# A hybrid decoder step on one core: how the sparse layer's lists are exchanged, and in which order its engines work

## The reference, cut to what matters

```python
q, k, v, iq, ik, iw = _split(h @ W['w_in_c'][j], C_SPLITS)
q = _rope(q.reshape(B, T, HC, DHC), pos)          # 8 heads of 128
k_rows = _rope(k.reshape(B, T, KVC, DHC), pos)    # 2 heads of 128
...
isc = jax.nn.relu(jnp.einsum('bthd,bsd->bths', iqb, ik_all))
isc = jnp.einsum('bths,bth->bts', isc, iwb)
isc = jnp.where((k_pos[None, :] <= qp[:, None])[None], isc, -jnp.inf)
top, sel = lax.top_k(isc, topk)                   # 256 of 1032 keys for a sample's token
...                                               # softmax attention over the chosen keys only
y = o.reshape(B, T, HC * DHC) @ W['w_out_c'][j]
```

## Time and profile before

| what | value |
|---|---|
| three runs | 2281.42, 2282.49 (median), 2288.36 us |
| the profiled execution | 2288.35 us, its span 2286.6 us |
| TensorE busy | 2117.3 us, 93% of the span |
| VectorE, ScalarE, POOL busy | 1233.7, 708.4, 269.7 us |
| chain that ended last, by engine | TensorE 72%, VectorE 12%, issue 5%, weight loads of TensorE 5%, ScalarE 3%, transfers 2% |
| mean granted clock of TensorE | 0.98 of full speed |

### The profile page before, as it was taken

One profiled execution on the slowest core, in us unless ns is written; L12 is line 12 of the kernel. 1 busy time (PEld: TensorE's weight loads), 2 busy tenths in 40 slices (PEclk: granted clock), 3 DMA queues, 4 the chain that ended last, 5 costly groups with the idle time before them and its releaser, 6 DMA issues.

```text
span 2286.6 us, 37435 instructions
## 1 busy us (share of the span) xinstructions
PE 2117.3 (93%) x15226; PEld 1873.6 (82%) x15230; DVE 1233.7 (54%) x2035; ACT 708.4 (31%) x1085; POOL 269.7 (12%) x243
## 2 busy tenths in 40 slices
PE   8988899898999999999998998888998999999997
PEld 6755697688878999999996576668976999999996
DVE  4367376855353566336634898564443466525642
ACT  5244334423231322212234424342322322212222
POOL 0022003431000000000003235220000100000001
PEclk9999999989999999999999999999999999999998
DMA  5378323314442222222224125642343222222221
GB/s 185 116 235 276 98 74 122 120 51 139 174 150 87 74 84 75 83 74 84 70 76 128 54 74 171 189 125 80 125 166 124 75 75 83 75 83 80 78 73 56
DMA packets 220861, 249.28 MB, mean 109 GB/s; under 512 B 18498, under 2 KB 175436, under 8 KB 220486
## 3 DMA queue, kind: packets, MB, share of 16 engines
q1 hardware_dynamic: 199162, 196.22, 27.1%
q0 software_dynamic: 9936, 28.78, 3.9%
q10 hardware_dynamic: 11592, 21.88, 2.8%
HBM read 233.63 MB, written 13.00 MB: 108 GB/s over the span
## 4 chain that ended last, share of the span: by engine, by line
PE 72%; DVE 12%; issue 5%; PEld 5%; ACT 3%; DMA 2%; PEldq 1%; POOL 0%; SPq 0%; DVEq 0%; POOLq 0%; ACTq 0%
PE PS L831 50%; PE PS L888 5%; PE PS L810 4%; PEld PS L831 2%; PE PS L1255 1%; PE PS L1270 1%; DVE arena L3202 1%; DVE arena L3200 1%; DVE arena L3235 1%; DVE arena L3232 1%; PE PS L1442 1%; DVE arena L2434 1%; PEld PS L1133 1%; PEld PS L810 1%; DVE stat L2527 1%
## 5 line engine op out<-in xcount | busy, mean ns | idle before, releaser
L831 PE MATMUL PS<-hT_r,WH 128*128 128x288 f32 (+2 forms) x1856 | 554.0, 298 | 21.7 <-issue 17.1
L831 PE MATMUL PS<-xr_r,WH 128*128 128x288 f32 (+2 forms) x1920 | 570.3, 297 | 1.6 <-POOL W_r L658 1.6
L831 PE MATMUL PS<-hT_r,W_r 128*128 128x288 f32 (+2 forms) x1856 | 549.5, 296 | 0.0
L2391 DVE TENSOR_TENSOR W_r<-W,WH 128x1024 fp32r<-128x1024 f32 (+1 forms) x219 | 284.2, 1317 | 373.0 <-ACT WH L1706 372.1
L831 PE MATMUL PS<-arena_r,WH 128*128 128x224 f32 (+2 forms) x1920 | 439.4, 297 | 3.7 <-issue 3.7
L1706 ACT ACTIVATE WH<-W 128x1024 fp32r<-128x1024 f32 (+1 forms) x262 | 266.1, 1034 | 504.6 <-PE PS L831 279.0
L831 PEld LDWEIGHTS PS<-hT_r,WH 128*128 128x128 f32 x1856 | 350.2, 189 | 35.0 <-issue 31.6
L831 PEld LDWEIGHTS PS<-xr_r,WH 128*128 128x128 f32 x1920 | 362.9, 189 | 2.3 <-issue 2.3
L831 PEld LDWEIGHTS PS<-hT_r,W_r 128*128 128x128 f32 x1856 | 350.3, 189 | 0.0
L831 PEld LDWEIGHTS PS<-arena_r,WH 128*128 128x128 f32 x1920 | 325.0, 189 | 6.4 <-issue 6.3
L831 PE MATMUL PS<-arena_r,W_r 128*128 128x288 f32 (+2 forms) x704 | 208.7, 296 | 0.0
(11 more groups left out here) (439 smaller groups left out, 3056.6 us busy)
## 6 DMA issues: line engine op xcount, KB each, us to landing
W<-in_w_ffn_in SPq DMA_DIRECT2D x176, 256.0 KB, 3.3
W<-in_w_ffn_out SPq DMA_DIRECT2D x40, 512.0 KB, 3.5
W<-in_w_in_ab SPq DMA_DIRECT2D x28, 512.0 KB, 3.6
C<-in_cache_mem_k SPq DMA_DIRECT2D x10, 1024.0 KB, 7.8
C<-in_cache_diff_k POOLq DMA_DIRECT2D x32, 256.0 KB, 3.9
C<-in_cache_diff_k SPq DMA_DIRECT2D x32, 256.0 KB, 3.4
C<-in_cache_diff_v POOLq DMA_DIRECT2D x32, 256.0 KB, 5.1
C<-in_cache_diff_v SPq DMA_DIRECT2D x32, 256.0 KB, 5.0
```

Source lines behind the costliest of these rows:

```text
L831: ins = mm(o, w[:, k, c * 128:c * 128 + 128], v(k0 + k)[:, t0:t1], start=opens and first and k == 0 and e == 0, stop=last and k == nk - 1 ...
L2391: v_.tensor_tensor(slot_view(WL, NW, n), slot_view(W, NW, n), plain(slot_view(WH, NV, n)), ALU.subtract).then_inc(lo_done, 1)
```

## The change

It touches only the order of work and the waits of the sparse stage.

1. `swap_lists` goes from POOL to SP, ahead of the first slot of the output weights, and so behind the first three key blocks. POOL makes its low halves without a stop.
2. The new keys are rotated after 18 rounds, not after 22.
3. ScalarE: `cp_turned(a + 1)` ahead of `cp_exp(a + 2)`.
4. VectorE: in the turns that load keys, the first key copy stands ahead of `cp_max(a)`, where that is there; the low half of an output slot (`ahead`) is made in the middle of the next turn, not at a turn's end, and there is one fewer before the end.
5. The barrier is gone. TensorE waits for all copies of turned tiles (`wait_tr`) and, at chunk 6 of the first block, for VectorE's last copy of values; ScalarE waits for its stores and for the last values before it fetches the memory keys. `align(NBANK, 3)` gives the first block the upper three of six banks.

```diff
 (SP)
+            def swap_lists():
+                sp.wait_ge(handoff["lists"], 1)
+                for e in range(2):
+                    sp.dma_start(L["tops_other"][64 * e:64 * e + 64], L["tops"][64 - 64 * e:128 - 64 * e]).then_inc(swapped, 16)
+
             for kind, n in LOADS:
                 if kind == "w":
+                    if n == first_slot["c_out"]:
+                        swap_lists()
...
 (POOL; the same function is taken away there)
                     a, z = POOL_RUNS[1]
-                    rests(a, z - 3)
-                    swap_lists()
-                    rests(z - 3, z)
+                    rests(a, z)
...
 (TensorE)
             cp_values(4 * (NB // 2) - 1, last)
-            barrier()
+            wait_tr()
             tj.use(6, 7)
-            project_features("c_out", oX_c, "D")
+            pj.align(NBANK, 3)
+
+            def pair_ready(k):
+                if k == 6:
+                    pe.wait_ge(handoff["p_copied"], DP + 4 * (NB // 2))
+
+            project_features("c_out", oX_c, "D", pair_ready)
...
 (ScalarE)
                     cs_keys(1, range(1), "DA")
+                cp_turned(a + 1)
                 cp_exp(a + 2)
-                cp_turned(a + 1)
...
-            barrier()
             tj.use(6, 7)
+            pj.align(NBANK, 3)
+            act.wait_ge(stores, 16 * S["stores"])
+            act.wait_ge(handoff["p_out"], DP + 4 * (NB // 2))
             fetch_memory(1)
...
 (VectorE)
-            largest(6, 22)
+            largest(6, 18)
...
-            largest(22, 32).then_inc(handoff["lists"], 1)
+            largest(18, 32).then_inc(handoff["lists"], 1)
...
-            def cs_keys(bb, groups, whos):
+            def cs_keys(bb, groups, whos, halves=range(2)):
                 for g in groups:
-                    for half in range(2):
+                    for half in halves:
...
                 a, more = 4 * p, p + 1 < NB // 2
+                if more:
+                    cs_keys(0, range(1), "DA", range(1))
                 if p:
                     cp_max(a)
                 if more:
-                    cs_keys(0, range(2), "DA")
+                    cs_keys(0, range(1), "DA", range(1, 2))
+                    cs_keys(0, range(1, 2), "DA")
...
                 cp_max(a + 1)
+                if p:
+                    ahead(first_slot["c_out"] + p - 1)
...
-                ahead(first_slot["c_out"] + p)
                 cs_turned(p)
             cp_copy(4 * (NB // 2) - 1)
-            barrier()
+            pj.align(NBANK, 3)
```

More of the change, by code:

```diff
@@ L659, in rests @@
                                             ALU.subtract).then_inc(lo_pool, 1)
[L661 to L664, removed]
             def sample_states():
```

## The result

The changed kernel took **2267.94 us** in the median of six runs (2265.68 to 2276.94), the kernel before, in the same rounds, 2286.12 (2281.42 to 2288.36): a ratio of **0.9938, 95% interval 0.9919 to 0.9958**. It is faster by 0.6%, and 2268.7 was forecast. The profiled execution took 2267.56 us, its span 2265.8, with a mean granted clock of 0.983.

A forecast was written before the change was run, and what follows sets the result against it. TensorE at its projections was taken as the bound, so only its standstills pay. Terms -8.0 + 1.0 - 5.4 + 2.0 - 1.5 - 1.9 gave -13.8 us, a forecast median of 2268.7 us, range 2264.5 to 2276.

The forecast's parts named there:

- The swap leaves POOL: Values' projection: TensorE loses its 4.06 us wait for POOL and 3.1 us of slow clock, together 7.2 us.
- the swap on SP: SP's queue: swap issued behind twelve key loads at 1427.9, lists in time, merge 0.5 us in place of 5.17.
- Rival B: List merge on VectorE is slow by itself, reading one list backwards; in all -8.6, 2273.9 us; chance 0.07.
- New keys rotated sooner: TensorE's new-key turn: rotating four rounds sooner saves 3.6 us of wait and slow clock; the rotation takes some 10 us.
- Start of the loop: Sample scores start at 1439.2, not 1447.22, after TensorE waits 2.8 us for the selection: -8.0 us.
- The clock's +1.0: Before the sample scores, TensorE's wait can lower the clock: 0 to +2.5 us, +1.0 taken.
- part 5: Attention loop: ScalarE's copies ahead of the next exponentials save 1.35 us in each of four turns, -5.4 us.
- VectorE's key copy first: Turns 1 and 2: maximum, exponentials and ScalarE's key copy come 1.0 us later, +2.0 us for both.
- The split moved: VectorE's weight split goes into a wait for keys, saving 0.8 us at two borders; taken as -1.5 us.
- no barrier: Before the output projection, TensorE's 2.09 us standstill nearly goes: -1.9 us.
- Rival D: Slower: the clock stays low through the loop after the wait before the sample scores; 2292 us; chance 0.04.
- E: Whole kernel: no change to be told, gains and losses cancel to within 6.8 us; chance 0.07.

The follow-up runs named there:

- experiment 2: Changed kernel with the new keys rotated after 22 rounds again, not 18; 2273.42 us, ratio 0.9950 to the kernel before.
- experiment 11: Changed kernel with the new keys rotated after 9 rounds, not 18, and nothing else; 2269.28 us, ratio 0.9930 to the kernel before.
- experiment 3: Changed kernel with ScalarE's exponentials of the next job ahead of its copies again; 2279.54 us, ratio 0.9973 to the kernel before.
- experiment 5: Changed kernel with VectorE's weight split back at the end of each turn; 2274.23 us, ratio 0.9947 to the kernel before.
- experiment 6: Changed kernel with the barrier back at the sparse stage's end and the align calls gone; 2273.70 us, ratio 0.9942 to the kernel before.
- experiment 4: Changed kernel with VectorE's maximum ahead of the first key copy again; 2270.99 us, ratio 0.9938 to the kernel before.
- experiment 9: Changed kernel measured again without an edit, the second execution; 2270.30 us, ratio 0.9922 to the kernel before.
- experiment 7: Kernel before with only the loop's edits: swap on POOL, new keys after 22 rounds; 2279.28 us, ratio 0.9964 to the kernel before.
- experiment 1: Changed kernel with the list swap back on POOL, ahead of its last three low halves; 2282.38 us, ratio 0.9976 to the kernel before.

## Why the prediction was right, step by step

1. *The swap leaves POOL* (7.2 us for TensorE) and 3. *the swap on SP.* Right. TensorE no longer stands in the projection, the swap is issued at 1423.13, just behind the twelfth key load, and the merge takes 0.42 us where 0.5 was expected. With parts 1 and 2 together TensorE was ready for the sample scores 10.1 us sooner, and 10.7 in the second execution (10.8 forecast). Rival B is out: the same instruction took 0.42 or 0.43 us beside an idle POOL (the eight executions, of seven kernels, that have the swap on SP behind the twelfth key load), 1.53 where one half that began at 1419.31 still ran, and 4.98, 5.17 and 5.32 beside three in a row. The reading of the merge as work plus waiting was taken from one pair of rows; it held.

2. *New keys rotated sooner.* Right in price (3.8 to 4.1 by experiment 2, 3.6 taken) and in course: start at 27.34 (27.4 forecast), 9.44 us long (10), lists 3.1 us later than before (4.1). The lists were then ready 1.87 us ahead of SP (1421.26 against 1423.13), so that their lateness was hidden, as said, and experiment 11 shows it from the other side.

4. *Start of the loop.* -8.13 us against -8.0, and -7.5 to -7.8 in the six other executions that start alike. TensorE waited 1.93 us for the selection in the profiled execution; the others waited 2.74 to 2.90 (2.8 forecast).

   **The clock's +1.0 is the term that was mis-sized.** The effect exists, but not in every execution. Seven executions have a wait of 2.74 to 2.90 us ahead of the sample scores. Four of them (experiments 3, 5, 6 and 11) have a stretch at 0.5, the 1.2 GHz level, that begins at the sample scores, and a turn 0 longer by 0.8 to 1.6 us; three (experiments 2, 4 and 9) have none. The profiled execution, with the shorter wait, had none either.

   What the sum put at nothing is the other low stretch, the one 6 to 11 us behind the start of the kernel before. It is gone: turn 0 lost 3.06 us, of which about 1.55 is part 5's copies and the other 1.5 the clock. In place of +1.0 stands -1.5, for this pair of executions. This stretch is there in both traces that have both of the old waits (the kernel before and experiment 7) and in none of the other eleven. With one of the two alone it is absent (experiment 1 has the wait for POOL, experiment 2 that in the new keys' turn). So it seems to go with the old start, but with one or two traces of each kind this is not shown.

5. *ScalarE's copies.* Predicted 1.35 a turn, measured 1.5: 3.53 less 1.98 is 1.55, and experiment 3 gives 1.52 and 1.52. For four turns -6.1 instead of -5.4.

6. *VectorE's key copy first.* Predicted +1.0 for each of turns 1 and 2, measured +0.94 and +0.98, by the mechanism named: the maximum, the exponentials and ScalarE's key copy shift in a row, and TensorE waits 1.79 us for the last.

7 and 8. *The split moved, no barrier.* -1.5 and -1.9, -3.4 together. Turn 1 is 0.57 shorter, which the copies and the key copy explain alone (-1.55 + 0.94). Turn 2 is 1.23 shorter: -1.55 + 0.98 leaves -0.66 for the split. Turn 3 is 4.19 shorter: -1.55 and another -0.66 leave -1.98 for the end. The sum of both parts is so -3.3. How the end divides was wrong: the barrier alone is 0.96, the rest goes with the split ahead of it.

The sum by the trace: -8.13 - 1.5 (clock) - 6.2 (copies) + 1.9 - 1.3 - 2.0 = -17.2, against -13.8. The difference of 3.4 is the clock with 2.5, the copies with 0.8 and rounding. The second execution of the changed kernel gives -13.6 with two low-clock stretches. That the forecast of 2268.7 is within 0.8 us of the median is partly luck: it rested on three runs of before with a median of 2282.49, six runs had 2286.12, and this difference of 3.6 us is as large as what the sum was short of. Rival D (a turn at low clock) did not occur in any of the twelve traces with the change or parts of it; the low stretches cost 0.8 to 1.7 us each. E is out by the interval.

**Open:** what decides whether a wait of 2 to 3 us lowers the clock in a given execution. Waits of 2.32 and 2.36 us in the new keys' turn were followed by 0.77 and 0.61. Of the seven waits of 2.74 to 2.90 us ahead of the sample scores four were followed by 0.5 and three by 1.00, the wait of 1.93 by 1.00, and within the turns the same code did both. No run isolated it.

## What to carry to other kernels

An instruction that is 5 us long beside another engine's work and ends where that work ends should be read as work plus waiting, and priced by the same form elsewhere in the trace; moving what it waits for is then worth more than shortening it. An edit that brings one engine forward lengthens every hand-made wait that another engine still has in its order, so move the two together, and after each gain look at the loading queue, since the next wait was there (2.58 us behind weights that nobody wanted yet). Where single stretches of clock move an execution by up to 1.7 us each, compare turn by turn from an anchor ahead of the first changed instruction, and not the ends of two spans.

## What the runs showed of the hardware that was not expected

- How long VectorE is held depends on the gaps between POOL's instructions, not only on the one it meets: the merge took 0.42 us beside none, 1.53 with one running, and about 5 beside three without a gap, where it got in at neither border. In the rotation, with gaps of 0.2 to 0.3 us between POOL's subtractions, each held instruction waited for one of them only (2.49, 2.30, 2.33 us beside 2.40 to 2.54), and the short ones ran in the gaps. The Trainium skill (SBUF — State Buffer, section "SBUF: two separate sides") has the loser of the shared ports blocked for the whole of one instruction; the rotation agrees, and the merge adds that a row of them without a gap blocks for the whole row.
- The rounds of MAX8 were not held at all: 0.76 us from 1417.19 to 1417.95, under POOL's subtraction of 1417.00 to 1419.40, and 0.76 us each beside its run of four from 1406.74. They read one input, the rotation and the merge two.
- The same kernel differs from itself by 3.6 us in this stage, 3.35 of it in two turns with low clock, and over its six runs from 2265.68 us, at a mean granted clock of 0.985, to 2276.94, at 0.980.
